# The first projection job of a hybrid-attention layer in two halves of 256 tokens, with the norm shared between engines

## The reference

```python
h = jnp.concatenate([meta, x], axis=1)
h = layer_norm(h, ln_emb_g, ln_emb_b)
...
proj = h @ w_in
(qa, ka, va, ga, qi, ki, wi, cq, ckv, kpe, gb) = jnp.split(proj, IN_OFFSETS, axis=-1)
...
qb = (rms_norm(cq, q_norm_g) @ w_uq).reshape(B, Lp, B_HEADS, B_NOPE + B_ROPE)
kvb = (rms_norm(ckv, kv_norm_g) @ w_ukv).reshape(B, Lp, B_HEADS, B_NOPE + B_V)
```

## Time and profile before

| | us |
|---|---|
| median of 3 runs | 345.21 (345.17 to 345.22) |
| the profiled execution, its own time | 343.74 |
| its span, first to last instruction | 341.9 |
| PE busy | 322.1 (94%) |
| DVE busy | 226.4 (66%) |
| POOL busy | 186.9 (55%) |
| ACT busy | 171.7 (50%) |

### The profile page before, as it was taken

The page is one execution under the profiler, slowest core; times in us unless marked ns, Lnnn a source line. Parts: engine busy times, 40 slices in busy tenths (PEclk is TensorE's granted clock), DMA queues, the critical chain, the costliest instruction groups (busy, mean ns, idle before and its releaser), DMA issues.

```text
span 341.9 us, 6103 instructions
## 1 busy us (share of the span) xinstructions
PE 322.1 (94%) x2130; PEld 271.5 (79%) x2130; DVE 226.4 (66%) x588; ACT 171.7 (50%) x378; POOL 186.9 (55%) x187
## 2 busy tenths in 40 slices
PE   0799999999999999999999999999999999999990
PEld 0488977788778888887887888797978897998990
DVE  6763120269966799988875985467677766444686
ACT  4774553354433455566434554667587753622221
POOL 4342999959322262256322578598659371650462
PEclk9999999999999999999999999999999999999997
DMA  7464343229423121201400132222333110130023
GB/s 274 174 202 161 123 126 124 92 66 291 148 69 113 47 94 61 71 20 58 133 2 15 63 117 102 71 88 92 96 93 95 63 63 0 63 125 0 3 100 146
DMA packets 11565, 32.86 MB, mean 96 GB/s; under 512 B 2392, under 2 KB 2392, under 8 KB 11536
## 3 DMA queue, kind: packets, MB, share of 16 engines
q1 hardware_dynamic: 8944, 27.08, 23.3%
q10 hardware_dynamic: 2592, 5.40, 5.4%
HBM read 29.83 MB, written 4.81 MB: 101 GB/s over the span
## 4 chain that ended last, share of the span: by engine, by line
PE 74%; DVE 17%; issue 3%; ACT 3%; DMA 2%; SPq 0%; DVEq 0%; ACTq 0%
PE ps_j L1273 42%; PE ps_o L1538 6%; PE ps_s L1483 4%; PE ps_s L1487 3%; DVE iw L1110 3%; DVE top L1106 3%; PE ps_t L1273 2%; PE ps_j L1325 2%; PE ps_t L1507 2%; PE ps_s L1454 2%; DMA res<-in_x 2%; DVE iw L1091 2%; PE ps_t L1512 2%; PE ps_j L1373 1%; DVE tmp L1063 1%
## 5 line engine op out<-in xcount | busy, mean ns | idle before, releaser
L561 POOL TENSOR_TENSOR wl<-raw,wh 128x1024 fp32r<-128x1024 f32 (+2 forms) x33 | 77.4, 2352 | 66.5 <-ACT wh L568 66.4
L1273 PE MATMUL ps_j<-hh,wh 128*128 128x512 f32 (+2 forms) x216 | 75.6, 350 | 0.1
L1273 PE MATMUL ps_j<-hl,wh 128*128 128x512 f32 (+2 forms) x216 | 74.8, 346 | 0.0
L1273 PE MATMUL ps_j<-hh,wl 128*128 128x512 f32 (+2 forms) x216 | 74.5, 345 | 0.0
L691 POOL TENSOR_SCALAR pr<-pr,rden 128x528 f32<-128x528 f32 (+1 forms) x64 | 35.2, 570 | 52.1 <-DVE rden L1152 52.1
L1273 PEld LDWEIGHTS ps_j<-hh,wh 128*128 128x128 f32 (+1 forms) x216 | 40.3, 186 | 6.5 <-issue 1.0
L1273 PEld LDWEIGHTS ps_j<-hl,wh 128*128 128x128 f32 (+1 forms) x216 | 40.3, 186 | 5.2 <-issue 0.2
L1273 PEld LDWEIGHTS ps_j<-hh,wl 128*128 128x128 f32 (+1 forms) x216 | 40.3, 187 | 5.1
L568 ACT ACTIVATE wh<-raw 128x1024 fp32r<-128x1024 f32 (+2 forms) x35 | 36.0, 1041 | 0.7 <-DMA raw<-in_weights 0.7
L703 POOL TENSOR_TENSOR bm<-bias,mask 128x144 f32<-128x144 f32 (+3 forms) x32 | 25.5, 835 | 0.0
L886 ACT ACTIVATE pr<-ps_s,mn 128x528 f32<-128x528 f32 (+3 forms) x32 | 16.9, 540 | 14.9 <-DVE mn L1138 14.9
(11 more groups left out here) (283 smaller groups left out, 816.5 us busy)
## 6 DMA issues: line engine op xcount, KB each, us to landing
raw<-in_weights SPq DMA_DIRECT2D x37, 512.0 KB, 3.7
bias_by_distance<-bias_vector ACTq DMA_DIRECT2D x1, 2624.0 KB, 12.7
bias<-bias_by_distance ACTq DMA_DIRECT2D x8, 264.0 KB, 2.9
res<-in_x SPq DMA_DIRECT2D x4, 512.0 KB, 4.9
out<-res SPq DMA_DIRECT2D x3, 512.0 KB, 2.6
pt<-in_ln_emb_g SPq DMA_DIRECT2D x1, 512.0 KB, 4.9
pt<-in_ln_emb_b SPq DMA_DIRECT2D x1, 512.0 KB, 6.5
q_b<-qpe ACTq DMA_DIRECT2D x8, 64.0 KB, 2.0
```

The source lines that it names most:

```text
L561: eng.tensor_tensor(ring_of(False, b), raw_of(b), ring_of(True, b).bitcast(F32), ALU.subtract).then_inc(done, 1)
L1273: last = pe.matmul(dst, a, b, start=n == 0 and part[0], stop=n == count - 1 and part[1])
```

## The change

- **Two halves.** The first job's unit of work is now two chunks by 256 tokens (`unit`): units 0 to 3 are the eight chunks of tokens 0 to 255 (tiles 0 and 1), units 4 to 7 those of tokens 256 to 511 (tiles 2 and 3). A unit has four transposes, eight matmuls against the high part (`high`) and four against the low part (`low`), all of 256 columns.
- **Norms.** GpSimd norms the meta tile, tile 0, and the right halves of tiles 1 to 3; ScalarE the left halves of tiles 1 to 3. VectorE takes each tile's statistics in two pieces, with other work between them.
- **Gain and shift.** In units 0, 1, 4 and 6 (`DIRECT`) ScalarE writes the high part straight from PSUM with gain and shift applied, and VectorE then applies them in PSUM for the low part. In the others ScalarE applies them in place and copies.
- **Weight blocks 0 and 1.** GpSimd rounds block 0 and VectorE block 1, each in two pieces; the low parts are made in four pieces.
- **Loads.** Token tile 3 is loaded after weight blocks 0 and 1.
- **Fillers.** TensorE makes 28 transposes of the identity into an unused bank as soon as the identity is there, and eight more behind the meta tile's. The bias table's matmuls stand ahead of the meta tile's transposes.
- **Sums of squares.** ScalarE writes the rounded square (`cqh`, `ckh`), VectorE the rest (`cql`, `ckl`), and TensorE sums both with fp32r ones.

```diff
-HIGH_BY_DVE = [b in (("cq", 0), ("cq", 1)) for b in BLOCKS]
+FIRST_BLOCKS = 2
+DIRECT = (0, 1, 4, 6)
+HIGH_AT = [sum(2 if n in DIRECT else 1 for n in range(u + 1)) for u in range(DC)]
...
+        ones = sb("ones", [P, P], F32R)
...
+        def unit(u):
+            i, a = u % 4, u // 4
+            return (2 * i, 2 * i + 1), slice(META + 256 * a, META + 256 * a + 256)
...
+            for t in range(QT - 1):
...
+                if b == 1:
+                    sp.dma_start(res[:, QT - 1, :], x[0, NQ - P:NQ, :]).then_inc(x_in[QT - 1], 16)
...
+            def normal(t, r, cols, need):
+                x_ = x_meta[:, cols] if t == 4 else res[:, t, cols]
+                pool.wait_ge(shift, need)
+                pool.tensor_scalar(x_, x_, mv[0:r, t, 0:1], rstd[0:r, t:t + 1], ALU.subtract,
+                                   ALU.mult).then_inc(xn_pool, 1)
+            def first_high(n):
+                pool.wait_ge(raw_in[0], 16)
+                c = slice(4 * n, 4 * n + 4)
+                pool.tensor_copy(wh[:, c, 0:P], raw[:, 0, c, :]).then_inc(w_high_pool, 1)
+            normal(4, META, slice(0, D), 1)
+            normal(0, P, slice(0, D), 2)
+            first_high(0)
+            normal(1, P, slice(512, D), 3)
+            first_high(1)
+            for n in range(4):
+                c = slice(2 * n, 2 * n + 2)
+                pool.wait_ge(w_high_pool, n // 2 + 1)
+                pool.wait_ge(w_high_dve, n // 2 + 1)
+                pool.tensor_tensor(wl[:, c, 0:2 * P].rearrange("p c (b n) -> p b c n", b=2), raw[:, 0:2, c, :],
+                                   wh[:, c, 0:2 * P].rearrange("p c (b n) -> p b c n", b=2).bitcast(F32),
+                                   ALU.subtract).then_inc(w_low, 1)
+            normal(2, P, slice(512, D), 5)
+            normal(3, P, slice(512, D), 7)
...
-            for n in range(6):
...
+            def normal(t, need):
+                act.wait_ge(shift, need)
+                act.activation(res[:, t, 0:512], res[:, t, 0:512], ACT.Identity, bias=nmr[:, t:t + 1],
+                               scale=rstd[:, t:t + 1]).then_inc(xn_act, 1)
+            def high(u):
+                chunks, s = unit(u)
+                act.wait_ge(x_t, u + 2)
+                for n, c in enumerate(chunks):
+                    half = hbank(u)[:, 256 * n:256 * n + 256]
+                    if u in DIRECT:
+                        act.activation(hh[:, c, s], half, ACT.Identity, bias=bcol[:, c:c + 1],
+                                       scale=gcol[:, c:c + 1]).then_inc(h_high, 1)
+                    else:
+                        act.activation(half, half, ACT.Identity, bias=bcol[:, c:c + 1],
+                                       scale=gcol[:, c:c + 1]).then_inc(h_aff_act, 1)
+                if u not in DIRECT:
+                    act.wait_ge(h_aff_act, 2 * sum(n not in DIRECT for n in range(u + 1)))
+                    act.activation(hh[:, chunks[0]:chunks[1] + 1, s], hbank(u).rearrange("p (c n) -> p c n", c=2),
+                                   ACT.Copy).then_inc(h_high, 1)
+            deviation(0)
+            deviation(1)
+            deviation(2)
+            normal(1, 4)
+            deviation(3)
             act.wait_ge(par_in, 32)
-            for c in range(DC):
-                if c % 2:
-                    act.wait_ge(x_t, c + 2)
-                    act.activation(hbank(c), hbank(c), ACT.Identity, bias=bcol[:, c:c + 1],
-                                   scale=gcol[:, c:c + 1]).then_inc(h_aff_act, 1)
-                    act.wait_ge(h_aff_act, c // 2 + 1)
-                else:
-                    act.wait_ge(h_aff, c // 2 + 1)
-                act.activation(hh[:, c, META:T], hbank(c), ACT.Copy).then_inc(h_high, 1)
-                if c == 3:
-                    high_part(act, 2)
+            high(0)
+            high(1)
+            high(2)
+            deviation(4)
+            normal(2, 6)
+            high(3)
+            normal(3, 8)
+            high(4)
+            high_part(act, 2)
+            high(5)
+            high(6)
+            high(7)
...
+                        act.wait_ge(job_act, BY_ACT[j + 1])
+                        act.activation(cqh[:, n, :], cq_t[:, n, :], ACT.Square).then_inc(sq_high, 1)
...
+            def first_high(n):
...
+                dve.tensor_copy(wh[:, c, P:2 * P], raw[:, 1, c, :]).then_inc(w_high_dve, 1)
+            def low(u):
+                chunks, s = unit(u)
+                dve.wait_ge(h_high, HIGH_AT[u])
+                if u in DIRECT:
+                    for n, c in enumerate(chunks):
+                        half = hbank(u)[:, 256 * n:256 * n + 256]
+                        dve.tensor_scalar(half, half, gcol[:, c:c + 1], bcol[:, c:c + 1], ALU.mult,
+                                          ALU.add).then_inc(h_aff, 1)
+                    dve.wait_ge(h_aff, 2 * sum(n in DIRECT for n in range(u + 1)))
+                c = slice(chunks[0], chunks[1] + 1)
+                dve.tensor_tensor(hl[:, c, s], hbank(u).rearrange("p (c n) -> p c n", c=2), hh[:, c, s].bitcast(F32),
+                                  ALU.subtract).then_inc(h_low, 1)
+            stat(0, 0)
+            stat(0, 1)
+            stat(1, 0)
+            inverse(0, 1)
+            stat(1, 1)
+            stat(2, 0)
+            inverse(1, 2)
+            stat(2, 1)
+            stat(3, 0)
+            inverse(2, 3)
+            stat(3, 1)
+            first_high(0)
+            first_high(1)
+            inverse(3, 5)
+            stat(4, 0)
+            dve.wait_ge(par_in, 32)
+            low(0)
+            stat(4, 1)
+            low(1)
+            inverse(4, 7)
+            low(2)
+            low(3)
...
-            for n in range(2):
-                dve.wait_ge(raw_in[n], 16)
...
+            for u in range(4, DC):
+                low(u)
...
+                        dve.wait_ge(squared, 2 * n + 1)
+                        dve.wait_ge(sq_high, n + 1)
+                        dve.tensor_tensor(cql[:, n, :], cq_sq[:, n, :], cqh[:, n, :].bitcast(F32),
+                                          ALU.subtract).then_inc(squared, 1)
...
+            def busy(count):
+                for _ in range(count):
+                    pe.transpose(ps_j[:, 1, 0:P], ident[:, :], ident[:, :])
...
-            pe.wait_ge(xn_done, 1)
+            busy(28)
+            pe.wait_ge(oh_in, 16)
...
+            busy(8)
+            def spread(u):
+                chunks, s = unit(u)
+                if u >= 4:
+                    pe.wait_ge(h_low, u - 3)
+                for n, c in enumerate(chunks):
+                    for k in range(2):
+                        a = 256 * n + P * k
+                        last = pe.transpose(hbank(u)[:, a:a + P], res[:, 2 * (u // 4) + k, c * P:(c + 1) * P], ident[:, :])
                 last.then_inc(x_t, 1)
-            for c in range(4):
-                spread(c)
+            def high(u):
+                chunks, s = unit(u)
+                a = 256 * (u // 4)
...
+                for n, c in enumerate(chunks):
+                    pe.wait_ge(h_high, HIGH_AT[u] - int(u in DIRECT and n == 0))
+                    for k in range(2):
+                        pe.matmul(ps_j[:, k, a:a + 256], wh[:, c, k * P:k * P + P], hh[:, c, s], start=c == 0, stop=False,
+                                  skip_group_check=True)
+                pe.wait_ge(w_low, u % 4 + 1)
+                for c in chunks:
+                    for k in range(2):
+                        pe.matmul(ps_j[:, k, a:a + 256], wl[:, c, k * P:k * P + P], hh[:, c, s], start=False, stop=False,
+                                  skip_group_check=True)
...
+            def low(u):
+                chunks, s = unit(u)
+                a = 256 * (u // 4)
+                pe.wait_ge(h_low, u + 1)
+                for k in range(2):
+                    for c in chunks:
+                        last = pe.matmul(ps_j[:, k, a:a + 256], wh[:, c, k * P:k * P + P], hl[:, c, s], start=False,
+                                         stop=c == DC - 1, skip_group_check=True)
+                    if u == DC - 1:
+                        last.then_inc(job_mm, 1)
+            pe.wait_ge(xn_pool, 2)
+            pe.wait_ge(xn_act, 1)
+            spread(0)
+            spread(1)
+            pe.wait_ge(xn_pool, 3)
+            spread(2)
+            spread(3)
+            high(0)
+            high(1)
+            low(0)
+            high(2)
+            low(1)
+            high(3)
+            pe.wait_ge(xn_act, 3)
+            spread(4)
+            low(2)
+            low(3)
+            spread(5)
+            high(4)
+            pe.wait_ge(xn_pool, 5)
+            spread(6)
+            high(5)
+            low(4)
+            spread(7)
+            high(6)
+            low(5)
+            high(7)
+            low(6)
+            low(7)
...
-                        pe.wait_ge(squared, 2)
+                        pe.wait_ge(squared, 4)
                         for c in range(2):
```

(7 more changed lines are left out.)

149 lines of the change are left out of this document (50 added, 99 removed).

## The result

| | us |
|---|---|
| the changed kernel, median of 12 runs | 347.35 (345.74 to 349.32) |
| the kernel before, 12 runs of the same chip | 345.19 (343.58 to 346.05) |
| ratio | 1.0072, 95% interval 1.0047 to 1.0097 |
| the profiled execution after, its own time | 348.49 (span 346.7) |

The ratio compares the two sets of executions whole; it is not the quotient of the two medians, which would give 1.0063. The forecast was 343.6. The change is 2.2 us slower by the medians.

The account below looks back on a forecast made before the run. TensorE was taken as the only bound; ckv 0.4 us earlier and sums of squares 1.2 us shorter gave -1.6 us, so 343.6 us against a median of 345.21, with a range of 341.6 to 346.0.

Parts of the forecast that it names:

- What bounds the kernel: Whole kernel: TensorE, busy 94% of the span, is the only bound from the first job on.
- Fillers: TensorE's start: 28 fillers cost nothing in idle time and bring the fast pace before 7 us.
- Kept: Gap between last starting filler and bias matmuls: TensorE's fast clock was assumed to survive about 2 us of idleness.
- Order of the loads: Load queue: what stood behind token tile 3 lands 1.5 us earlier, bias inputs at 8.4 instead of 9.9.
- Start of the transposes: First real transpose at 10.9 instead of 13.40, with GpSimd's norm of tile 0 done by 9.7 at worst.
- Rival 2: Clock lost before the bias matmuls: slow transposes at about 13.4, ckv at 32.2, total 346.1 us; chance 0.15.
- TensorE's work: First job: 32 transposes take 3.5 us and 96 matmuls of 256 columns 11.4 us.
- Waits inside: First job: six TensorE waits for half-size operations at units and before ckv, 3.9 us in sum.
- ckv at 29.6: ckv's first matmul, after the first job, comes at 29.6 instead of 30.01, 0.4 us earlier.
- Sums of squares: Matmuls as fp32r instead of fp32: 1.72 us becomes 0.93 and 0.89 becomes 0.50, 1.2 us saved.
- new work beside it: Added Squares, subtractions and GpSimd's low parts cost nothing; block 3 keeps 1.0 us of slack before kk.
- rival 4: Block 3 late or GpSimd's queue mispriced: a wait of 1 to 2 us at kk, about 345; chance 0.05.

Follow-up runs that it names:

- a_act: The change with every norm on ScalarE instead of GpSimd: 346.04 us, 1.0029 of the kernel before.
- p_one: The change with GpSimd's norm multiplying by one column and constant 1.0, mean not subtracted: 345.0 us, one execution.
- a_fill: The change with 27 instead of 8 fillers behind the meta tile's transposes: 347.08 us, 1.0069 of the kernel before.
- p_muladd: The change with GpSimd's norm as multiply and add instead of subtract and multiply: 347.21 us, one execution.
- p_forms: The change with a different form of GpSimd's operation in each tile, norm not computed rightly: 345.76 us, one execution.
- muladd_only: The change with GpSimd's norm as multiply and add, still 28 fillers, in more executions: 1.0012 of the kernel before.
- the bridge: 46 instead of 28 fillers at the start, up to the bias matmuls: worth 0.4%, 1.3 us, where GpSimd's norm doesn't hold TensorE up.
- bridge_only: The change with 46 instead of 28 fillers at the start, its subtracting norm kept: 1.0053 of the kernel before.
- muladd_bridge: The change with GpSimd's norm as multiply and add and 46 fillers at the start: 0.9973 of the kernel before.
- muladd_order: The change with multiply-add norm, 46 starting fillers, and block 2's high part on ScalarE moved behind unit 6: 343.03 us, 0.9949 of the kernel before.
- a_nofill: The change without any filler: 346.95 us, 1.0068 of the kernel before.

## Why the prediction was wrong, point by point

- *What bounds the kernel.* "After the start nothing longer than 0.6 us" misreads the waits: the earlier trace rows has 1.16 and 1.02 us between the first instruction and the transposes. It holds from 17 us on, and the sum uses it only there.
- *Fillers.* They bring TensorE to the fast pace before 7 us, as taken. The bias matmuls behind the gap were fast in the profiled executions of the change, of a_act, p_one and a_fill (2.02, 1.88, 2.40 and 2.92 us idle), and slow in those of p_muladd, p_forms and muladd_only (2.62, 2.34 and 1.98). In a_fill the clock fell later, in unbroken work. "Kept" was right for some executions and wrong as an average; the bridge's 1.3 us measures it. The length of the gap doesn't sort the seven. How long the 28 fillers took does: 4.79 to 5.00 us in the four, 5.05 to 5.61 in the three, so the pace held where TensorE had turned fast earlier ahead of the gap. The margin is thin, and no run tests it. The Trainium skill ("TensorE: Matmul & The Clock Gate", section "HAM oscillation") describes a kernel with bursts of about 2 us and DMA waits of about 3 to 5 us between them, in which every burst starts at the half rate. The gaps here are shorter, and three of seven ended so.
- *Order of the loads.* Right for the change: bias inputs at 8.31 against 8.4. In the other executions with this order of loads they land between 8.2 and 9.3, so the 8.4 was near the early end.
- *Start of the transposes.* **This is the step that failed**: "so 1024 some 1.4 us, and even at the 2.35 us of a two-input operation of that width it would end at 9.7". The norm takes 3.76 us, it waits behind the meta tile's norm of the same length, which I had not put into GpSimd's queue at all, and it ends at 12.98. My row was a GpSimd scale by one column; it held for a multiplication and said nothing of a subtraction. The bounds were taken from rows of other operations, and no row showed this one. I should have kept a bound further out.
- *What followed from it.* Rival 2's consequence, slow transposes, came true, but with a wait that the forecast did not have. In the change the bias matmuls ran fast, and the clock fell 0.3 us into the wait for GpSimd; bridge_only shows that this wait can cost it alone, a_fill that it can fall without it. In the change the fast pace came back at 21.7. Rival 2's ckv of 32.2 became 34.9. Rival 2 as it was written is seen in muladd_only: transposes slow at 13.51 (13.4 there), first matmul at 16.68 (16.1), ckv at 32.92 (32.2).
- *TensorE's work.* Right: 14.9 forecast, 15.0 in the accounting above.
- *Waits inside.* With the norm mended these are the best part of the forecast. 0.3, 1.1, 0.4, 1.0, 0.5 and 0.6 were forecast; muladd_bridge prints 0.26, 0.76, 0.29, 0.90, 0.40 and 0.54, at the places named. The half-width affine on ScalarE takes 0.51 to 0.55 (0.53 taken from the 256-column row). But a stop costs more than the idle time that the row prints: in muladd_order 14.70 to 15.64 is 0.94 for work of 0.47, with 0.27 printed. Summed from start to start the six stops of muladd_bridge, whose order is the forecast's, are 4.4, with 3.15 printed; those of muladd_order are 3.9, with 2.7 printed. So the places and the idle times were right, and the sum of 3.9 was 0.5 short for the forecast's order.
- *ckv at 29.6.* With the mend 31.3. Its start, 11.9 in place of 10.9, is one us of that: the bias inputs land at 9.1 there, not 8.4. Another 0.5 is what the stops cost beyond 3.9, and 0.2 is left in the work, some 0.1 at a change from transposes to matmuls (0.55 from start to start for the first four, 0.47 for the next).
- *Sums of squares, new work beside it.* Right: 0.93 and 0.49, no wait at kk. GpSimd's low parts end at 21.1, not 16.1, and even so block 3 was in time: rival 4 did not come.
- *The range.* 347.35 lies outside 346.0. The failure had a bound of 2.35 us where 3.76 stood twice.

Which of the 1.1 us between 62 us and the end belongs to the change, and why the bias inputs land up to 1 us apart between executions of one kernel, stays open: no run was made for either.

## What to carry to other kernels

When work moves to an engine on which the trace shows no such operation, measure that operation alone first, or let the bound be several times the nearest row; and put every instruction of that engine's queue into the sum, the small ones too, since the norm of the 16-row tile took as long as that of a 128-row tile (3.77 and 3.76 us). Write a norm as multiply and add. Fillers pay only if what follows them is ready: between a filler and real work there may be no gap, and a filler that holds work back costs what it saves. Compare kernels like these by many executions and their mean clocks, since one profile can be of either group. Test the parts of a bundled change one by one on the old kernel: here one part (the split sums) held all of the gain that the intervals can tell.

## What the runs showed of the hardware

- GpSimd's tensor_scalar with a subtraction takes 3.69 to 3.77 us for 1024 columns (3.93 once, in a_fill) and 1.93 to 2.07 for 512, whether it is the first or the second operation, on a column or a constant. With multiplications and additions it takes 1.11 to 1.19 for 1024 and 0.69 to 0.77 for 512. GpSimd's operations on two tensors show nothing of the kind: for 1024 columns a subtraction takes 2.35 us, and in the kernel before a multiplication (L661) 2.45 and an addition (L664) 2.39.
- After an idle stretch of about 2 to 3 us on TensorE at the start, the next matmuls are slow in some executions and fast in others of nearly the same program (1.98, 2.34 and 2.62 slow; 1.88, 2.02, 2.40 and 2.92 fast).
- The clock can fall in the midst of unbroken work: in a_fill at about 11.7, 2.4 us after the idleness had ended.
- In the change the slow pace lasted from the transposes at 13.04 to 21.69 with one stop of 0.65 us in it; in bridge_only, with the same stop, it was over by 19.28, having begun at 13.47. In the kernel before it was over by 17.04, 3.6 us after 13.40, with no stop.
- The printed granted clock can read 1.00 at the half pace: over the first slow stretch of the kernel before, and in a_nofill until 20.9, where four matmuls take 0.85 us from start to start. So its mean, 0.995 to 0.996 in a_nofill, doesn't prove the fast pace; the pace from start to start does.
- A stop of TensorE between matmuls costs some 0.2 us more than the idle time that its row prints. The printed idleness begins at the modelled end of the last matmul; in muladd_order that is 15.37, where the pace would have had the next matmul start at 15.17.
